# Expert rounds of 32 token slots on four column strips of TensorE, in place of 64 slots on two

## The reference

```python
top_v, top_i = lax.top_k(logits, TOP_K)
top_w = jax.nn.softmax(top_v, axis=-1)
comb = jnp.sum(jax.nn.one_hot(top_i, N_EXPERTS) * top_w[..., None], axis=1)
gate = jnp.minimum(jnp.einsum('td,edf->tef', t, w_gate) + b_gate, 7.0)
up = jnp.clip(jnp.einsum('td,edf->tef', t, w_up) + b_up, -7.0, 7.0)
act = (up + 1.0) * gate * jax.nn.sigmoid(1.702 * gate) * comb[..., None]
out = jnp.einsum('tef,efd->td', act, w_down) + comb @ b_down
```

## Time and profile before

| | |
|---|---|
| median of 3 runs | 1342.5 us (1340.11 to 1344.37) |
| profiled execution, first to last instruction | 1338.4 us |
| mean granted TensorE clock | 0.941 of full speed |
| TensorE busy | 1137.8 us (85%) |
| VectorE, ScalarE, GpSimd busy | 419.2, 178.2, 153.8 us |
| read from HBM | 444.60 MB |

### The profile page before, as it was taken

One profiled execution on the slowest core, in us unless ns is written; L12 is line 12 of the kernel. 1 busy time (PEld: TensorE's weight loads), 2 busy tenths in 40 slices (PEclk: granted clock), 3 DMA queues, 4 the chain that ended last, 5 costly groups with the idle time before them and its releaser, 6 DMA issues.

```text
span 1338.4 us, 17170 instructions
## 1 busy us (share of the span) xinstructions
PE 1137.8 (85%) x6470; PEld 476.7 (36%) x6471; DVE 419.2 (31%) x952; ACT 178.2 (13%) x273; POOL 153.8 (11%) x172
## 2 busy tenths in 40 slices
PE   1215964997699999988999999999999999999984
PEld 1114643854233333333333333333333333333321
DVE  6997388214312211122211211122112211221113
ACT  1111210212111111111111111111111111111111
POOL 3992276002100000000000000000000000000000
PEclk9767986998599999999999999999999999999997
DMA  7630287254299999999999999999999999999993
GB/s 163 276 125 1 62 246 302 104 217 176 104 401 409 410 409 409 410 410 409 397 410 410 409 410 409 406 410 409 409 410 410 409 398 409 410 409 410 410 410 135
DMA packets 117827, 446.46 MB, mean 334 GB/s; under 512 B 8734, under 2 KB 9110, under 8 KB 117702
## 3 DMA queue, kind: packets, MB, share of 16 engines
q1 hardware_dynamic: 116998, 444.35, 84.6%
q0 software_dynamic: 480, 1.13, 0.5%
q10 hardware_dynamic: 320, 0.57, 0.1%
HBM read 444.60 MB, written 1.44 MB: 333 GB/s over the span
## 4 chain that ended last, share of the span: by engine, by line
PE 44%; SPq 27%; DVE 18%; DMA 7%; issue 3%; ACT 1%; DVEq 0%; POOL 0%; ACTq 0%
SPq L426 26%; PE ps L949 18%; PE ps L977 11%; DMA ring<-in_w_up 7%; DVE gm L1171 3%; PE ps L906 2%; PE ps L848 2%; PE ps L600 2%; PE ps L793 2%; DVE tmpg L1171 2%; PE ps L717 2%; DVE bbx L1263 2%; PE ps L833 1%; DVE actT L1532 1%; DVE upc L1522 1%
## 5 line engine op out<-in xcount | busy, mean ns | idle before, releaser
L949 PE MATMUL ps<-ring,XT 128*64 128x512 f32 x2240 | 497.0, 594 | 18.4 <-DMA ring<-in_w_gate 9.9
L949 PEld LDWEIGHTS ps<-ring,XT 128*64 128x64 f32 x2240 | 159.3, 137 | 331.7 <-issue 290.3
L977 PE MATMUL ps<-ring,actT 128*64 128x512 f32 x1120 | 248.1, 595 | 4.5
L1520 DVE TENSOR_SCALAR gcl<-ps 128x512 f32<-128x512 f32 x35 | 24.2, 692 | 344.5 <-PE ps L949 344.5
L977 PEld LDWEIGHTS ps<-ring,actT 128*64 128x64 f32 x1120 | 77.4, 137 | 152.7 <-issue 137.9
L1522 DVE TENSOR_SCALAR upc<-ps 128x512 f32<-128x512 f32 x35 | 24.2, 692 | 294.0 <-PE ps L949 294.0
L906 PE MATMUL ps<-h,sel 128*64 128x512 f32 x288 | 69.7, 605 | 4.0 <-DVE sel L1488 4.0
L925 PE MATMUL ps<-ys,selT 64*128 64x512 f32 x288 | 71.5, 615 | 0.7 <-ACT ys L1146 0.7
L600 PE MATMUL ps<-cst,gm 128*128 128x128 f32 x48 | 8.9, 360 | 62.3 <-DVEq L1273 61.2
L1144 ACT COPY selT<-ps 128x256 f32<-128x256 f32 x35 | 13.1, 373 | 361.7 <-PE ps L600 361.7
L1141 ACT ACTIVATE sgm<-gcl 128x512 f32<-128x512 f32 x35 | 22.1, 630 | 230.0 <-DVE gcl L1520 230.0
(11 more groups left out here) (275 smaller groups left out, 975.1 us busy)
## 6 DMA issues: line engine op xcount, KB each, us to landing
ring<-in_w_gate SPq DMA_DIRECT2D x64, 2048.0 KB, 21.6
ring<-in_w_up SPq DMA_DIRECT2D x64, 2048.0 KB, 21.9
ring<-in_w_down SPq DMA_DIRECT2D x64, 2048.0 KB, 23.3
ring<-in_w_ada SPq DMA_DIRECT2D x12, 2048.0 KB, 11.6
ring<-in_w_in SPq DMA_DIRECT2D x2, 2048.0 KB, 11.0
wout<-in_w_out SPq DMA_DIRECT2D x1, 4096.0 KB, 13.9
wglu<-in_s_w_glu SPq DMA_DIRECT2D x1, 2304.0 KB, 18.2
cst<-in_constants SPq DMA_DIRECT2D x1, 784.0 KB, 4.8
```

The lines of the kernel that those rows point to most:

```text
L949: ins = pe.matmul(out[64 * fh:64 * fh + 64, :], XT[:, k % 4, (k // 4) * 64:(k // 4) * 64 + 64], w(i)[:, k % 4, fh * HALF:(fh + 1) * HALF], ...
L977: ins = pe.matmul(pX[64 * dh:64 * dh + 64, :], actT[:, k % 4, (k // 4) * 64:(k // 4) * 64 + 64], w(i)[:, k % 4, dh * HALF:(dh + 1) * HALF] ...
```

## The change

A round takes 32 slots. The array is split in four column strips of 32; each holds the same slots and streams one quarter (256 columns, `QU`) of the weight rows. A PSUM result is 128 partitions (4 quarters x 32 slots) x 256, and all tiles of a round (`Xs`, `gcl`, `sgm`, `upc`, `acts`, `ys`) have 256 columns instead of 512. The transposes are two for activations, two for tokens and two for the weighted selection (before: four, four, two). The down product and the transposes get PSUM places of their own (`pY`, `pA`, `pS`), and a wait for `ys_ready` before `gather` goes. The output of both token halves lies in four banks, one for each quarter; the last multiply and add are four instructions of 1024 columns. Loads, ring and the rules of release are the same.

The diff, without the lines that only move tiles in SBUF:

```diff
--- before.py
+++ after.py
@@ -32,10 +32,11 @@
 NE = 32
-SL_ = 64
+SL_ = 32
 NR = NE + 4 * 2 * L // SL_
...
 HALF = 512
+QU = D // 4
 MODW = 256
@@ -207,17 +208,17 @@
...
-        XT = at("XT", G_OFF + 2048, [P, 4, P])
-        actT = at("actT", G_OFF + 12288, [P, 4, P])
+        XT = at("XT", G_OFF + 1024, [P, 2, P])
+        actT = at("actT", G_OFF + 6144, [P, 2, P])
-        selw = at("selw", G_OFF + 16384 + 512, [P, 2, 2, SL_])
+        selw = at("selw", G_OFF + 16384 + 256, [P, 2, 4, SL_])
...
@@ -280,8 +281,9 @@
-        OUT = [[ps[:, 2 * tau + dh, :] for dh in range(2)] for tau in range(2)]
-        pG, pU, pX, pT = (ps[:, b, :] for b in (4, 5, 6, 7))
+        OUT = [[ps[:, dq, tau * QU:(tau + 1) * QU] for dq in range(4)] for tau in range(2)]
+        pG, pU, pX, pY = (ps[:, b, 0:QU] for b in (4, 5, 6, 7))
+        pA, pS, pT = (ps[:, b, QU:2 * QU] for b in (4, 5, 6))
@@ -902,16 +904,16 @@
                 for tau in range(2):
-                    for dh in range(2):
-                        ins = pe.matmul(pX[64 * dh:64 * dh + 64, :], sel[:, tau, :],
-                                        h2[:, tau, dh * HALF:(dh + 1) * HALF], start=(tau == 0), stop=(tau == 1),
+                    for dq in range(4):
+                        ins = pe.matmul(pX[32 * dq:32 * dq + 32, :], sel[:, tau, :],
+                                        h2[:, tau, dq * QU:(dq + 1) * QU], start=(tau == 0), stop=(tau == 1),
                                         skip_group_check=True)
...
                 pe.wait_ge(sem("Xs_ready"), r + 1)
-                for n in range(4):
+                for n in range(2):
                     ins = tr(pT[:, n * P:(n + 1) * P], Xs[:, n * P:(n + 1) * P])
@@ -920,9 +922,9 @@
                 for tau in range(2):
-                    for dh in range(2):
-                        rows = slice(64 * dh, 64 * dh + 64)
-                        ins = pe.matmul(OUT[tau][dh], selT[rows, tau * P:(tau + 1) * P], ys[rows, :],
+                    for dq in range(4):
+                        rows = slice(32 * dq, 32 * dq + 32)
+                        ins = pe.matmul(OUT[tau][dq], selT[rows, tau * P:(tau + 1) * P], ys[rows, :],
                                         start=False, stop=False, skip_group_check=True)
@@ -938,44 +940,42 @@
-                    for fh in range(2):
-                        pe.matmul(out[64 * fh:64 * fh + 64, :], selb[:, :], bias3[:, m, fh * HALF:(fh + 1) * HALF],
+                    for fq in range(4):
+                        pe.matmul(out[32 * fq:32 * fq + 32, :], selb[:, :], bias3[:, m, fq * QU:(fq + 1) * QU],
                                   start=True, stop=False, skip_group_check=True)
...
                             pe.wait_ge(unit_in[i], 16 * e + 16)
-                        for fh in range(2):
-                            ins = pe.matmul(out[64 * fh:64 * fh + 64, :], XT[:, k % 4, (k // 4) * 64:(k // 4) * 64 + 64],
-                                            w(i)[:, k % 4, fh * HALF:(fh + 1) * HALF], start=False,
+                        for fq in range(4):
+                            ins = pe.matmul(out[32 * fq:32 * fq + 32, :], XT[:, k % 2, (k // 2) * 32:(k // 2) * 32 + 32],
+                                            w(i)[:, k % 4, fq * QU:(fq + 1) * QU], start=False,
                                             stop=(k == KD - 1), skip_group_check=True)
...
                     if m == 0:
-
-                        pe.wait_ge(sem("ys_ready"), R + 1)
                         gather(R + 1)
...
                 pe.wait_ge(sem("act_ready"), R + 1)
-                for n in range(4):
-                    ins = tr(pG[:, n * P:(n + 1) * P], acts[:, n * P:(n + 1) * P])
+                for n in range(2):
+                    ins = tr(pA[:, n * P:(n + 1) * P], acts[:, n * P:(n + 1) * P])
                 ins.then_inc(sem("act_turned"), 1)
...
                 for tau in range(2):
-                    ins = tr(pU[:, tau * P:(tau + 1) * P], selw[:, tau, :, :].rearrange("p a b -> p (a b)"))
+                    ins = tr(pS[:, tau * P:(tau + 1) * P], selw[:, tau, :, :].rearrange("p a b -> p (a b)"))
                 ins.then_inc(sem("sel_turned"), 1)
...
                         pe.wait_ge(unit_in[i], 16 * e + 16)
-                    for dh in range(2):
-                        ins = pe.matmul(pX[64 * dh:64 * dh + 64, :], actT[:, k % 4, (k // 4) * 64:(k // 4) * 64 + 64],
-                                        w(i)[:, k % 4, dh * HALF:(dh + 1) * HALF], start=(k == 0), stop=(k == KD - 1),
+                    for dq in range(4):
+                        ins = pe.matmul(pY[32 * dq:32 * dq + 32, :], actT[:, k % 2, (k // 2) * 32:(k // 2) * 32 + 32],
+                                        w(i)[:, k % 4, dq * QU:(dq + 1) * QU], start=(k == 0), stop=(k == KD - 1),
                                         skip_group_check=True)
@@ -986,9 +986,9 @@
             for tau in range(2):
-                for dh in range(2):
-                    ins = pe.matmul(OUT[tau][dh], combT[:, tau * P:(tau + 1) * P], bdn[:, dh * HALF:(dh + 1) * HALF],
-                                    start=True, stop=False, skip_group_check=True)
+                for dq in range(4):
+                    ins = pe.matmul(OUT[tau][dq], combT[:, tau * P:(tau + 1) * P], bdn[:, dq * QU:(dq + 1) * QU],
+                                    start=(tau == 0), stop=False, skip_group_check=True)
             ins.then_inc(sem("combT_used"), 1)
@@ -1141,9 +1141,9 @@
                 act.wait_ge(sem("sel_turned"), R + 1)
-                act.copy(selT[:, :], pU[:, 0:2 * P]).then_inc(sem("selT_ready"), 1)
+                act.copy(selT[:, :], pS).then_inc(sem("selT_ready"), 1)
                 act.wait_ge(unit_used[5], R + 1)
-                act.copy(ys[:, :], pX).then_inc(sem("ys_ready"), 1)
+                act.copy(ys[:, :], pY).then_inc(sem("ys_ready"), 1)
             for tau in range(2):
@@ -1493,9 +1493,9 @@
                 for tau in range(2):
-                    for n in range(2):
-                        ins = dve.tensor_scalar(selw[:, tau, n, :], slots, rank[:, tau, bass.ds(e, 1)],
-                                                comb[:, tau, bass.ds(e, 1)], ALU.is_equal, ALU.mult)
+                    ins = dve.tensor_scalar(selw[:, tau, :, :], slots.unsqueeze(1).broadcast_to([P, 4, SL_]),
+                                            rank[:, tau, bass.ds(e, 1)], comb[:, tau, bass.ds(e, 1)],
+                                            ALU.is_equal, ALU.mult)
                 ins.then_inc(sem("selw_ready"), 1)
@@ -1529,7 +1529,7 @@
                 dve.wait_ge(sem("act_turned"), R + 1)
-                dve.tensor_copy(actT[:, :, :], pG.rearrange("p (n x) -> p n x", x=P)).then_inc(sem("actT_ready"), 1)
+                dve.tensor_copy(actT[:, :, :], pA.rearrange("p (n x) -> p n x", x=P)).then_inc(sem("actT_ready"), 1)
                 dve.wait_ge(sem("X_turned"), R + 2)
@@ -1538,11 +1538,10 @@
             for tau in range(2):
-                for dh in range(2):
-                    tt(Xs[:, :], OUT[tau][dh], g2s[:, dh * HALF:(dh + 1) * HALF], ALU.mult)
-                    x = x_tok[:, tau, dh * HALF:(dh + 1) * HALF]
-                    tt(x, x, Xs[:, :], ALU.add)
-                    dve.sem_inc(sem("x3_ready"), 1)
+                o = h2[:, tau, :].rearrange("p (q c) -> p q c", q=4)
+                tt(o, ps[:, 0:4, tau * QU:(tau + 1) * QU], g2s[:, :].rearrange("p (q c) -> p q c", q=4), ALU.mult)
+                tt(x_tok[:, tau, :], x_tok[:, tau, :], h2[:, tau, :], ALU.add)
+                dve.sem_inc(sem("x3_ready"), 2)
             norm_scale(3)
```

More of the change, by code:

```diff
@@ L207, in build @@
         cT = at("cT", T_OFF + 2752 + 3072, [P, 16])
-        Xs = at("Xs", G_OFF, [P, HALF])
-        XT = at("XT", G_OFF + 2048, [P, 4, P])
-        gcl = at("gcl", G_OFF + 4096, [P, HALF])
-        sgm = at("sgm", G_OFF + 6144, [P, HALF])
-        upc = at("upc", G_OFF + 8192, [P, HALF])
-        acts = at("acts", G_OFF + 10240, [P, HALF])
-        actT = at("actT", G_OFF + 12288, [P, 4, P])
-        ys = at("ys", G_OFF + 14336, [P, HALF])
+        Xs = at("Xs", G_OFF, [P, QU])
+        XT = at("XT", G_OFF + 1024, [P, 2, P])
+        gcl = at("gcl", G_OFF + 2048, [P, QU])
+        sgm = at("sgm", G_OFF + 3072, [P, QU])
+        upc = at("upc", G_OFF + 4096, [P, QU])
+        acts = at("acts", G_OFF + 5120, [P, QU])
+        actT = at("actT", G_OFF + 6144, [P, 2, P])
+        ys = at("ys", G_OFF + 14336, [P, QU])
         sel = at("sel", G_OFF + 16384, [P, 2, SL_])
-        selw = at("selw", G_OFF + 16384 + 512, [P, 2, 2, SL_])
-        selb = at("selb", G_OFF + 16384 + 1536, [96, SL_], BF16)
+        selw = at("selw", G_OFF + 16384 + 256, [P, 2, 4, SL_])
+        selb = at("selb", G_OFF + 16384 + 1280, [96, SL_], BF16)
         selT = at("selT", T_OFF + 5120, [P, 2 * P])
@@ L230, in build @@
         cnt = at("cnt", MISC + 1888, [NE, 8])
-        cmp = at("cmp", MISC + 1920, [NE, 52])
-        brt_f = at("brt_f", MISC + 2944, [1, 64])
```

(6 more changed lines are left out.)

## The result

| | before | after |
|---|---|---|
| median of the runs | 1341.3 us (4 runs) | 1387.9 us (1386.98 to 1391.33, 4 runs) |
| ratio after/before | | 1.0357 (95% interval 1.0335 to 1.0379) |
| profiled span | 1338.4 us | 1385.0 us |
| mean granted clock | 0.941 | 0.888 |
| TensorE busy | 1137.8 us | 983.0 us |

The changed kernel is 3.6% slower, 46.6 us, where 26 were forecast. First the page of the kernel after, parts 2 and 3 (lines of the instruction queue from both pages, the one with 20 packets is the kernel's before); they answer to the earlier trace rows.

A forecast was written before the change was run, and what follows sets the result against it. The weight stream, 942 us, was taken as the bound; holes +30.1, start -3.0, end -3.2 and clock +2.0 gave +25.9 us on the 1338.4 us span, 1364, and a median of 1368 us, range 1352 to 1390.

The forecast's parts named there:

- Bound: Weight loads into the ring: 184 units at 409.6 GB/s, 942 us, set the end; TensorE's rounds are 9 us below.
- The rival of a faster stream: Weight stream in the loop: the lighter array lets it run at 419 GB/s, giving 1347 us; chance 7%.
- Length of a round: TensorE's full round falls from 26.66 to 14.0 us (13.5 to 15.2).
- The hole behind a three-round expert: Weight stream at experts 9, 16, 23: full ring delays the next issue, 10.9 us each, +30.1 us net in all.
- L: Time at which an expert's second gate unit, g1, is there and TensorE takes it at once.
- the threshold: Weight issue behind an expert: at L + 27.4 it just keeps the queue fed; each later microsecond is lost.
- the rival of a clock that stays low: TensorE at 1.2 GHz through a three-round expert's second round: 44 us more for the three, 1414 us; chance 8%.
- Number of rounds: Expert loop: 32 slots need 51 rounds against 35; experts 9, 16 and 23 take three.
- Two rounds: no hole, 3.1 us: Weight stream at two-round experts: the issue comes at L + 24.3, no hole, 3.1 us of cover.
- holes behind two-round experts: Weight stream: a sign that would make the prediction wrong; no such holes were forecast.
- a partly low clock: TensorE's clock falling in part between 1.2 and 2.4 GHz: up to +20 us, the upper side of the range.
- Start and end: Stream's first issue -3.0 us (-1 to -4); work behind the last weights -3.2 us (0 to -4).

The follow-up runs named there:

- e3: Changed kernel with TensorE's 32 experts written out and at most two rounds per expert (tokens beyond the 64th left out): 1345.8 us, 1.0029 of the kernel before.
- e1: Changed kernel with TensorE's loop over groups of four experts written out as 32 experts in a row: 1380.5 us, 1.0286 of the kernel before.
- e4: Kernel before (64 slots, two strips) with its loop written for eight experts instead of four: 1354.0 us, 1.0091 of the kernel before.
- e5: Kernel before (64 slots, two strips) with its 32 experts written out in TensorE's program: 1351.5 us, 1.0081 of the kernel before.
- e9: Changed kernel with a weight ring of nine places and loops of three experts, two experts behind: 1352.5 us, 1.0056 of the kernel before.
- e10: Kernel before (64 slots, two strips) with a weight ring of nine places and loops of three experts: 1337.2 us, 0.9952 of the kernel before.

## Why the prediction was right in sign and short in size

**Bound.** Right. Outside the dips the stream stays at 408 to 409 GB/s; TensorE's busy time fell by 155 us, and all that the time gained from the faster rounds are the 6.5 us at the start and the end. e3, without third rounds and jumps back, comes out within 0.3% of the kernel before. The rival of a faster stream is out: with TensorE idle much more, no slice of the kernel after passes 409. (Its threshold was a little off: 30 us of 942 take 423.1 GB/s, not 422.3. Nothing hangs on it.)

**Length of a round.** Right: 14.08 against 14.0. Scatter's row strips do run side by side (16 instructions in 1.15 us), and the clamps take 0.42.

**The hole behind a three-round expert.** Right in place and mechanism, nearly in size. The issue came at L + 38.5 at expert 23 where L + 38.3 was worked out. The three holes sum to 38.0 for 32.7. About 1 us of each is the threshold: read as L + 27.4, it was L + 26.5 (38.5 - 12.0). At expert 16 the last down half ran in 3.45 us instead of 1.93 (granted clock 0.54 there), which is 1.5 of the 2.4 us by which this hole is larger; the rest isn't explained. The clock's share was thus rightly small, and e1's remainder of 1.0 at the same place agrees; the rival of a clock that stays low is out, since in the rounds that decide it is 1.00.

**Where it failed.** The step *Number of rounds* and the one-line cover of *Two rounds: no hole, 3.1 us* treat a round as data and products only. The sum has no term for the program itself. Four strips double TensorE's instructions: a round has 238 products and as many weight loads for 126 and 126. Four experts of code no longer stay held, and two costs come in. One is a wait of 7 us at each of seven jumps back, which opens holes at two-round experts 4 and 24, 3.3 and 7.9 of the 12.1 us of other holes. The other is the code's own transfers through the same DMA engines, most of the +5.8 spread thinly. e1 and e4 show the first from both sides: without jumps back the stream lost 9.5 us less. e5 and e9 show the second; but e9 and e10, with 9 and 5 transfers left, still lose 2.4 and 1.9 thinly where the kernel before loses 1.1, so about 1 us of the 5.8 has no cause shown. Other holes and thin loss are together 17.9 of the 20.7 us that were missing; the rest is the size of the three holes (+3.2), the start (+1.1) and the end (-1.4).

The Trainium skill has the rule that I didn't weigh: "Runtime: NRT & Kernel Launch", section "Instruction fetch mechanics", says that TensorE's instruction memory of 128 KiB (2048 instructions) is refilled in blocks of 16 KiB, and that a taken branch to code outside the current window of two blocks stops the engine until it is fetched. The trace agrees in kind: the packets are of 16 KB, and by products and loads alone the loop bodies are 4 x 252 = 1008 instructions (before, held), 3 x 476 = 1428 (e9, held), 4 x 476 = 1904 (after, not held) and 8 x 252 = 2016 (e4, not held), to which waits and register instructions come. By an estimate from e1, whose 61 transfers of 16 KB in the rounds brought 32 x 476 products and loads, these four bodies take some 66, 94, 125 and 132 KB. So the window of two blocks doesn't fit: bodies of 66 and 94 KB are held. The measurement decides.

**Its own signs.** The prediction named holes behind two-round experts as a sign of being wrong, and they came. Two more of its signs came out off: TensorE idled 150 us for weights (56.9, 36.9 and 56.4 in the groups above) and not some 200, and of the 28 slices only 11 are at 409 GB/s and 8 at 408. That 1387.9 still lies inside 1352 to 1390 is luck: the upper side was kept for a partly low clock, up to +20, and what filled it was the code.

**Start and end.** The start brought 1.9 for 3.0: the stream's start varied by some 3 us among profiles with the same front part, so this term was below what one profile tells. The end brought 4.6 for 3.2: the last down half ran at the full clock, and VectorE's last part took 5.1 us from first start to last end instead of 6.1, 1.0 less where 0.4 was taken (instructions of 1226 ns, not 1285).

## What to carry to other kernels

Where a stream of weights is the bound, compute time counts only through the release of its buffers: time the **last** use of the oldest buffer against the lead of the ring, expert by expert, and not the sum of work. A cut that doubles the instructions of a looped body has a price in code: look at the instruction queue's packets in the steady part and at idle time with no releaser at the first instruction behind a jump back. More lead was worth more than a faster round: one more place in the ring made the kernel before 6 us faster (e10), rounds of 14.1 us for 26.7 with their third rounds and longer code made it 46.6 us slower.

## What the hardware showed that I had not expected

Jumps back cost 6.8 to 7.5 us each with a loop of 1904 products and loads, 3.8 to 4.3 with one of 2016 in the two-strip kernel, about 1 us with 1428. Where the code isn't held, 3.3 to 3.5 us of this pass between the end of the 16 KB packet and the first product. A 16 KB code transfer, 0.04 us of bandwidth at 409.6 GB/s, cost the stream 0.08 to 0.12 us (the rise of the thin loss over the extra transfers, in the kernel after, e1, e3, e4 and e5). The packet records agree in kind: such a packet took 1.07 us on its DMA engine, where four weight packets of 4 KB would take 0.65; a sixteenth of 1.07 is 0.07. Four row strips of 32 scatter at 0.05 to 0.07 us an instruction (16 in 1.15 us with the last one's tail).
